# Order of weight products in pairs, split lag products and a new placing of intra-block products in a one-core encoder layer

## The chip, the cores and the metric

The kernel runs on one core of one Trainium2 chip. The metric is the device time of one execution in microseconds (us). The engines are TensorE (PE, with its weight loads shown apart as PEld), VectorE (DVE), ScalarE (ACT), GpSimd (POOL) and SyncE (SP), whose queue issues most DMAs.

## What is computed

One encoder layer on 256 tokens of width 2048, float32 throughout:

```python
q, k, v, u, g_att, g_ssm = jnp.split(x @ w_in, splits, axis=-1)   # 8 heads x 128; u: 64 groups x 16
y_att = neighbourhood_attention(q, k, v, rpb) @ w_na_out
y_s = s5_scan(u, forward) + s5_scan(u, reverse) + d * u            # 64 complex states per group
y_s = gelu(y_s); y_s = y_s * sigmoid(y_s @ w_glu + b_glu)
mix = (sigmoid(g_att + b) * y_att + sigmoid(g_ssm + b) * (y_s @ w_s5_out)) @ w_out
h = layer_norm(ALPHA * x + mix)
out = layer_norm(ALPHA * h + (silu(h @ w_gate) * (h @ w_up)) @ w_down)
```

## The kernel before

**Weights.** All weights come as one stream of tiles of 128x1024 floats. SP loads each into one of six slots of `raw` (`load`, line 328). ACT rounds it into one of four slots of `whi` (`split_hi`, line 580, the copy in line 585), and DVE writes the remainder, raw minus whi, over the raw tile as `wlo` (`split_lo`, line 1065, line 1068). Activations are kept in the same two parts, so a product is high x both parts plus low x high part.

**The product of a tile.** `prod_w` (lines 1727 to 1740) takes a tile as eight 128x128 stationary blocks: eight matmuls of 512 columns with `whi` (line 1734), then a wait for the tile's `wlo`, then eight of 256 columns with `wlo` (line 1738), into one PSUM bank. The last one raises `w_used`, on which three things wait: SP's load six tiles later, ACT's `split_hi` four tiles later, and the copies of the finished bank. An output of the input projection, or of the feed-forward's gate or up projection, takes two such tiles, one for each half of the 2048 inputs. `prod_b` (line 1742) and `prod_b_rows` (line 1755) use the activations as the stationary operand, 12 matmuls of 512 columns to a tile (lines 1750 to 1752, and 1769 to 1771).

**Stages in order.** The u projection (16 tiles, `U_ORDER`), the v projection (16 tiles, `prod_b`), the loop over eight heads `f` with `PER_F` = 12 tiles each (q, k and gates; lines 1919 to 1944), 40 tiles of branch projections, 32 of the output projection, layer norm with transposes (`h_part`, `h_pair`), the feed-forward's gate and up tiles (first twelve in `FF_ORDER`, then `ff(m)`, line 2057), 88 down tiles and the last norm.

**The state-space layer in the loop.** Time is cut into `Q` = 4 positions j of a block and `NB` = 64 blocks. Head f's step has three bursts of small float32 matmuls, placed by hand among the tiles j of the loop; each matmul of the code is two in the trace, called passes here:
- `s5_in(f)` (line 1850): 32 matmuls with 64 rows, 64 columns of weights, 64 columns streamed, on all four 64x64 positions of the array.
- `blocks(f)`: the kernels for lags -3 to 3. 16 matmuls (line 1829) with 128 rows and 32 weight columns, 7 lags x 16 = 112 columns streamed, into the four 32-partition strips of bank `WB`; rows 0 to 63 hold the forward direction and rows 64 to 127 the reverse one, and `cp` is zero where a direction has no lag. Then four small ones with the diagonal term (line 1832).
- `s5_out(f)`: eight matmuls within the blocks (line 1865), g = 0 on rows 0 to 63 and output partitions 0 to 63, g = 1 on rows 64 to 127 and partitions 64 to 127, then 32 with the block states (line 1874) on all four positions.

`s5_in(f+1)` and `blocks(f+1)` stand behind tile j = 10 of head f, `scores` and `s5_out` behind j = 7, `transposes` behind j = 11, `attend` behind j = 1 (for the last head, 5, 7, 9 and 10). ACT's `keep_lags` (line 645) copies the lags, ACT stores them and `y4` (`store_y`, two DMAs), and SP brings the lags back as `tb` (`stage_tb`). Everything on ACT and DVE is in an order written out by hand around the splits.

**Layer norm to feed-forward.** ACT runs `gain_even` (line 979), `pair_hi` (line 986) and the splits, DVE `gain_odd` (line 1593), `pair_low` (line 1072) and its own; `split_hi(0, H_FF + 4)` stands behind `pair_hi(5)` and `gain_even(7)`.

Of the kernel before, what the change touches and what calls it, by code (L numbers as in the profile page):

```python
# [28 lines left out]
P = 128  # L29
# [89 lines left out]
def build(nc, wstream, xT, xtok, b_rows, b_states, c_rows, d_rows, params, bias, cols, lnrows, out):  # L119
    ctx = ExitStack()  # L120
    with ctx:
# [84 lines left out]
        hi_ready, lo_ready, w_used = sem("hi_ready"), sem("lo_ready"), sem("w_used")  # L206
# [99 lines left out]
        def from_blocks(v):  # L306

            return v.rearrange("p (j r b) -> p b j r", j=Q, r=ROWS)

# [269 lines left out]
        def _(act):  # L579
            def split_hi(m, c):  # L580

                act.wait_ge(raw_landed[c % RING], 32 * m + 16 * (c // RING + 1))
                if not (isinstance(m, int) and 12 * m + c < HIS):
                    act.wait_ge(w_used, 12 * m + (c - HIS + 1))
                act.activation(whi[:, c % HIS, :], raw[:, c % RING, :], ACT.Copy).then_inc(hi_ready, 1)  # L585
# [54 lines left out]
            def keep_lags(f):  # L640
# [4 lines left out]
                act.activation(lags[:, :, :].rearrange("p m n -> p (m n)"), ps[WB][:, 0:7 * GC], ACT.Copy).then_inc(w_evac, 1)  # L645
                act.wait_ge(w_evac, f + 1)
# [4 lines left out]
            def store_y(f):  # L651

                act.wait_ge(fin_step, f + 1)
                for g in range(2):
                    act.dma_start(y_dram[f, :, GC * g:GC * g + GC, :],
                                  y4[64 * g:64 * g + 64, f % 2, :, :].rearrange("p q n -> p (q n)")).then_inc(y_stored, 16)

            def cross_y(f):

                act.wait_ge(y_done, f + 1)  # L660
                if f >= 2:
                    act.wait_ge(y_stored, 32 * (f - 1))
                act.activation(y4[:, f % 2, :, :].rearrange("p q n -> p (q n)"), y_bank(1), ACT.Copy).then_inc(y_cross, 1)

            def load_y(f):

                act.wait_ge(y_stored, 32 * f + 32)
# [396 lines left out]
        def _(dve):  # L1064
# [559 lines left out]
            split_lo(0, H_FF + 1)  # L1624
            gain_odd(4)
            split_lo(0, H_FF + 2)
# [93 lines left out]
        def _(pe):  # L1720
# [6 lines left out]
            def prod_w(m, c, act, k0, kn, bank, start, stop, ready=None, parts=False):  # L1727

                sh, sl = c % HIS, c % RING
                for i in range(kn):  # L1730
# [3 lines left out]
                    pe.matmul(bank[:, :], whi[:, sh, i * P:(i + 1) * P], both, start=start and i == 0, stop=stop and i == kn - 1,  # L1734
                              skip_group_check=parts)
                wait_split(m, c)
                for i in range(kn):
                    mm = pe.matmul(bank[:, 0:T], wlo[:, sl, i * P:(i + 1) * P], act[:, k0 + i, 0, :], start=False,  # L1738
                                   stop=stop and i == kn - 1, skip_group_check=True)
                mm.then_inc(w_used, 1)  # L1740

            def prod_b(c, act, k0, banks, start, stop):

                sh, sl = c % HIS, c % RING
                for n in range(2 * TT):
# [5 lines left out]
                    pe.matmul(banks[t][:, :], a, lo, start=False, stop=False)  # L1751
                    mm = pe.matmul(banks[t][:, :], b, hi, start=False, stop=stop and i == 1)  # L1752
                mm.then_inc(w_used, 1)

            def prod_b_rows(c0, act, k0, banks, between):

                for t in range(TT):
                    for m in range(SPL):
# [4 lines left out]
                        for i in range(2):  # L1763
# [6 lines left out]
                            pe.matmul(banks[t][:, :], a, lo, start=False, stop=False)  # L1770
                            mm = pe.matmul(banks[t][:, :], b, hi, start=False, stop=m == SPL - 1 and i == 1)  # L1771
                        if t == 1:
                            mm.then_inc(w_used, 1)
# [18 lines left out]

            pe.wait_ge(warm_ready, 1)
            keep_busy(ps[7], 7)
            for j, (n, h) in enumerate(U_ORDER):
                if h == 0:
                    wait_bank(N_U + n)
                if j == 0:
                    pe.wait_ge(half_hi, 1)
                else:  # L1800
                    wait_high(0, j)
                prod_w(0, j, act16, 8 * h, 8, ps[bank_of(N_U + n)], h == 0, h == 1,
                       x_split if n == 0 else None)
# [10 lines left out]
            def blocks(f):  # L1814
# [3 lines left out]
                else:  # L1818
                    pe.wait_ge(w_evac, f)
# [34 lines left out]
            def s5_out(f):  # L1854
# [7 lines left out]
                for q in range(4):  # L1862
# [317 lines left out]
```

## Time and profile before

| | us |
|---|---|
| median of 3 runs | 1366.38 (1365.68 to 1366.5) |
| the profiled execution's own time | 1366.87 |
| its span, first to last instruction | 1365.0 |
| PE busy in it | 1352.7 |
| DVE, ACT busy | 952.0, 680.9 |

The span is what the trace covers. Rows of the timeline give the start of a group in us from the span's start, how long it lasts until its last instruction ends, the engine, the line, the operation with its tiles and shape, and the count; an idle time before it with what ended it stands in brackets. Matmuls are pipelined: a matmul's duration overlaps that of the next, so the pace is read from start to start.

### The profile page before, as it was taken

To read this page: it belongs to the slowest core of one execution; us is meant where nothing else is said; L and a number is where in the kernel's file an instruction comes from. 1 tells how busy PE (TensorE), PEld (TensorE's weight loads), DVE (VectorE), ACT (ScalarE), POOL (GpSimd) and SP (SyncE) were. 2 spreads that over 40 slices of the span, in tenths; PEclk is the share of its full clock that TensorE was granted. 3 is DMA by queue.
4 is the path that set the end of the run, shared out by engine and by line. 5 is a ranking of instruction groups with operands and counts; after the bars stand their busy time and mean duration, and the time that the engine had idled before them with its cause. 6 is when DMAs were issued, how large, how long until landed. Compare 5 with 4: busy or idle time off the path is not lost.

```text
span 1365.0 us, 22724 instructions
## 1 busy us (share of the span) xinstructions
PE 1352.7 (99%) x8542; PEld 1164.4 (85%) x8542; DVE 952.0 (70%) x1291; ACT 680.9 (50%) x995; POOL 137.2 (10%) x207
## 2 busy tenths in 40 slices
PE   8999999999999999999999999999999999999998
PEld 7888888888888888888888888888888888888886
DVE  7989999999877797557666665555555554545454
ACT  5444555555548855347444444444444444333332
POOL 1842222220000000000222220000000000000001
PEclk9999999999999999999999999999999999999999
DMA  9667777676656676654656566566765666666663
GB/s 321 206 239 254 232 233 225 214 224 195 188 172 190 219 278 189 196 178 157 191 185 187 186 193 188 185 187 188 230 185 186 186 194 190 198 187 198 189 196 123
DMA packets 100797, 275.14 MB, mean 202 GB/s; under 512 B 25970, under 2 KB 33138, under 8 KB 100340
## 3 DMA queue, kind: packets, MB, share of 16 engines
q1 hardware_dynamic: 87364, 264.66, 61.5%
q10 hardware_dynamic: 9520, 5.54, 1.3%
q0 software_dynamic: 3840, 3.94, 1.0%
q8 instruction: 49, 0.80, 0.2%
q14 instruction: 24, 0.20, 0.1%
HBM read 268.12 MB, written 5.96 MB: 201 GB/s over the span
## 4 chain that ended last, share of the span: by engine, by line
PE 90%; DVE 6%; DMA 1%; SPq 1%; issue 1%; ACT 1%; DVEq 0%; ACTq 0%
PE bank L1734 41%; PE bank L1738 21%; PE bank L1750 8%; PE bank L1751 8%; PE bank L1752 8%; DVE wlo L1068 2%; DMA raw<-wstream 1%; DVE scratch L1094 1%; PE bank L1874 1%; PE bank L1850 1%; PE bank L1829 0%; PE bank L1771 0%; PE bank L1769 0%; PE bank L1770 0%; DVE scratch L1091 0%
## 5 line engine op out<-in xcount | busy, mean ns | idle before, releaser
L1068 DVE TENSOR_TENSOR wlo<-raw,whi 128x1024 fp32r<-128x1024 f32 x463 | 579.3, 1253 | 193.3 <-ACT whi L585 187.5
L585 ACT ACTIVATE whi<-raw 128x1024 fp32r<-128x1024 f32 x463 | 488.1, 1055 | 238.9 <-PE bank L1752 189.4
L1734 PE MATMUL bank<-act,whi 128*128 128x512 f32 x2280 | 575.8, 394 | 2.7 <-DVE act L1072 2.1
L1734 PEld LDWEIGHTS bank<-act,whi 128*128 128x128 f32 x2280 | 409.5, 189 | 78.6 <-DVE act L1072 4.1
L1738 PEld LDWEIGHTS bank<-act,wlo 128*128 128x128 f32 x2280 | 310.8, 190 | 25.4 <-DVE wlo L1068 3.2
L1738 PE MATMUL bank<-act,wlo 128*128 128x256 f32 x2280 | 318.1, 282 | 2.0 <-DVE wlo L1068 2.0
L1750 PE MATMUL bank<-whi,mid 128*128 128x512 f32 x340 | 132.3, 389 | 0.0
L1751 PE MATMUL bank<-wlo,mid 128*128 128x512 f32 x340 | 132.3, 389 | 0.0
L1752 PE MATMUL bank<-whi,mid 128*128 128x512 f32 x340 | 132.3, 389 | 0.0
L1654 DVE TENSOR_TENSOR usum<-bank,usum 128x256 f32<-128x256 f32 x44 | 18.7, 425 | 91.5 <-ACT usum L915 91.5
L915 ACT ACTIVATE usum<-bank 128x256 f32<-128x256 f32 x44 | 16.9, 384 | 126.9 <-PE bank L1738 126.9
L908 ACT ACTIVATE gsum<-bank 128x256 f32<-128x256 f32 x44 | 16.9, 384 | 118.8 <-PE bank L1738 118.8
L1750 PEld LDWEIGHTS bank<-whi,mid 128*128 128x128 f32 x340 | 63.8, 188 | 13.3
L1751 PEld LDWEIGHTS bank<-wlo,mid 128*128 128x128 f32 x340 | 63.8, 188 | 13.2
L1752 PEld LDWEIGHTS bank<-whi,mid 128*128 128x128 f32 x340 | 63.8, 188 | 13.2
L549 POOL DMA_DIRECT2D lrow<-lam_dram x120 | 57.1, 484 | 168.7 <-DVE tmp L1243 150.9
L1750 PE MATMUL bank<-whi,act 128*128 128x512 f32 x180 | 70.6, 392 | 0.2 <-DVE wlo L1068 0.2
L1751 PE MATMUL bank<-wlo,act 128*128 128x512 f32 x180 | 70.1, 389 | 0.0
L1752 PE MATMUL bank<-whi,act 128*128 128x512 f32 x180 | 70.1, 389 | 0.0
L1648 DVE TENSOR_TENSOR gsum<-bank,gsum 128x256 f32<-128x256 f32 x44 | 18.7, 425 | 69.2 <-ACT gsum L908 69.2
L563 POOL TENSOR_TENSOR hp<-hp,lnrow 128x512 f32<-128x512 f32 x8 | 18.8, 2348 | 410.6 <-DVE ev L1658 410.6
L573 POOL TENSOR_TENSOR hp<-hp,lnrow 128x512 f32<-128x512 f32 x2 | 2.5, 1266 | 538.6 <-ACT hp L1054 538.6
(200 smaller groups left out, 1158.9 us busy)
## 6 DMA issues: line engine op xcount, KB each, us to landing
raw<-wstream SPq DMA_DIRECT2D x463, 512.0 KB, 3.6
bt<-b_rows SPq DMA_DIRECT2D x8, 512.0 KB, 6.0
lrow<-lam_dram POOLq DMA_DIRECT2D x120, 32.0 KB
lnrow<-lnrows SPq DMA_DIRECT2D x3, 1024.0 KB, 7.0
xraw<-xT SPq DMA_DIRECT2D x8, 256.0 KB, 6.3
bs<-b_states SPq DMA_DIRECT2D x8, 256.0 KB, 5.4
hp<-xtok SPq DMA_DIRECT2D x4, 512.0 KB, 4.7
bm<-bias SPq DMA_DIRECT2D x8, 160.0 KB, 4.2
```

What stands on the lines that cost most here:

```text
L549: pool.dma_start(lrow[64 * g + j:64 * g + 64:Q, d, :, :, :].rearrange("p q r n -> p (q r n)"), row.to_broadcast([GC, 512])).then_inc(lrow_ ...
L563: pool.tensor_tensor(v, v, lnrow[:, 0, b], ALU.mult).then_inc(h_step, 1)
L585: act.activation(whi[:, c % HIS, :], raw[:, c % RING, :], ACT.Copy).then_inc(hi_ready, 1)
L908: act.activation(gsum[:, b, :], ps[bank_of(N_FF + 2 * i)][:, T:2 * T], ACT.Copy).then_inc(g_cross, 1)
L1068: dve.tensor_tensor(wlo[:, c % RING, :], raw[:, c % RING, :], whi[:, c % HIS, :].bitcast(F32), ALU.subtract).then_inc(lo_ready, 1)
L1648: dve.tensor_tensor(gsum[:, b, :], ps[bank_of(N_FF + 2 * i)][:, 0:T], gsum[:, b, :], ALU.add).then_inc(g_summed, 1)
L1654: dve.tensor_tensor(usum[:, b, :], ps[bank_of(N_FF + (2 * i + 1) % 6)][:, 0:T], usum[:, b, :], ALU.add).then_inc(u_summed, 1)
L1734: pe.matmul(bank[:, :], whi[:, sh, i * P:(i + 1) * P], both, start=start and i == 0, stop=stop and i == kn - 1, skip_group_check=parts)
L1738: mm = pe.matmul(bank[:, 0:T], wlo[:, sl, i * P:(i + 1) * P], act[:, k0 + i, 0, :], start=False, stop=stop and i == kn - 1, skip_group_che ...
L1750: pe.matmul(banks[t][:, :], a, hi, start=start and i == 0, stop=False)
L1751: pe.matmul(banks[t][:, :], a, lo, start=False, stop=False)
L1752: mm = pe.matmul(banks[t][:, :], b, hi, start=False, stop=stop and i == 1)
```

## The change

`prod_w` is cut into `high` (eight matmuls with `whi`, raising a new semaphore `hi_used`) and `low` (eight with `wlo`, raising `w_used`). In the head loop and in `ff` both tiles of an output are taken together: high, high, low, low. ACT's `split_hi` waits for `hi_used` and `lo_ready` instead of `w_used`. `blocks` takes each direction's three lags with 64 rows, into two banks, and the middle lag (zero) with all rows. `s5_out` places the products within the blocks of q = 2, 3 crosswise, so that they use all four positions. Three orders change: `s5_in` and `blocks` stand between the highs and the lows of the last pair, `split_hi(0, H_FF + 4)` and `split_lo(0, H_FF + 2)` stand earlier.

```diff
@@ lines 310 to 312
+        def y_rows(g, q):
+
+            h = g if q < 2 else 1 - g
+            return slice(64 * h, 64 * h + 64)
+
+        def lag_bank(f, d):
+
+            return ps[YB if f else AB][:, T:T + 3 * GC] if d else ps[WB][:, 4 * GC:7 * GC]
+
@@ split_hi, lines 582 to 585
-                    act.wait_ge(w_used, 12 * m + (c - HIS + 1))
+                    act.wait_ge(hi_used, 12 * m + (c - HIS + 1))
+                    act.wait_ge(lo_ready, 12 * m + (c - HIS + 1))
@@ keep_lags, lines 642 to 649
-                act.activation(lags[:, :, :].rearrange("p m n -> p (m n)"), ps[WB][:, 0:7 * GC], ACT.Copy).then_inc(w_evac, 1)
-                act.wait_ge(w_evac, f + 1)
+                act.activation(lags[:, Q - 1:2 * Q - 1, :].rearrange("p m n -> p (m n)"), ps[WB][:, 3 * GC:7 * GC], ACT.Copy).then_inc(w_evac, 1)
+                act.activation(lags[:, 0:Q - 1, :].rearrange("p m n -> p (m n)"), lag_bank(f, 1), ACT.Copy).then_inc(w_evac, 1)
+                act.wait_ge(w_evac, 2 * f + 2)
@@ store_y, lines 654 to 656
-                    act.dma_start(y_dram[f, :, GC * g:GC * g + GC, :],
-                                  y4[64 * g:64 * g + 64, f % 2, :, :].rearrange("p q n -> p (q n)")).then_inc(y_stored, 16)
+                    for q in (0, 2):
+                        act.dma_start(y_dram[f, :, GC * g:GC * g + GC, q * NB:q * NB + 2 * NB],
+                                      y4[y_rows(g, q), f % 2, q:q + 2, :].rearrange("p q n -> p (q n)")).then_inc(y_stored, 16)
@@ ACT, lines 990 to 995
                 pair_hi(g)
+                if g == 4:
+                    split_hi(0, H_FF + 4)
                 if g < 6:
                     gain_even(g + 2)
-                if g == 5:
-                    split_hi(0, H_FF + 4)
@@ DVE, lines 1624 to 1628
             split_lo(0, H_FF + 1)
+            split_lo(0, H_FF + 2)
             gain_odd(4)
-            split_lo(0, H_FF + 2)
@@ prod_b, lines 1750 to 1753 (prod_b_rows alike)
                     pe.matmul(banks[t][:, :], a, hi, start=start and i == 0, stop=False)
-                    pe.matmul(banks[t][:, :], a, lo, start=False, stop=False)
-                    mm = pe.matmul(banks[t][:, :], b, hi, start=False, stop=stop and i == 1)
-                mm.then_inc(w_used, 1)
+                    if n < 2 * TT - 1:
+                        pe.matmul(banks[t][:, :], a, lo, start=False, stop=False)
+                    mm = pe.matmul(banks[t][:, :], b, hi, start=False, stop=stop and n == TT)
+                mm.then_inc(hi_used, 1)
+                pe.matmul(banks[t][:, :], a, lo, start=False, stop=stop).then_inc(w_used, 1)
@@ blocks, lines 1826 to 1830
-                            pe.matmul(ps[WB][32 * q:32 * q + 32, 0:7 * GC], bs[:, r, 4 * g + q, :], cp[:, f % 2, r, 4 * g + q, :, :],
-                                      start=g == 0 and r == 0, stop=False, skip_group_check=True)
+                            for d in range(2):
+                                h = slice(64 * d, 64 * d + 64)
+                                c = cp[h, f % 2, r, 4 * g + q, (0 if d else Q):(Q - 1 if d else 2 * Q - 1), :]
+                                pe.matmul(lag_bank(f, d)[32 * q:32 * q + 32, :], bs[h, r, 4 * g + q, :], c.rearrange("p j n -> p (j n)"),
+                                          start=g == 0 and r == 0, stop=d == 1 and g == 1 and r == 1, skip_group_check=True)
+                for g in range(2):
+                    for r in range(2):
+                        for q in range(4):
+                            pe.matmul(ps[WB][32 * q:32 * q + 32, 3 * GC:4 * GC], bs[:, r, 4 * g + q, :], cp[:, f % 2, r, 4 * g + q, Q - 1, :],
+                                      start=False, stop=False, skip_group_check=True)
@@ s5_out, lines 1862 to 1866 (line 1874 writes to y_rows(g, q) too)
-                for q in range(4):
+                for q in (0, 2, 1, 3):
                     for g in range(2):
                         h = slice(64 * g, 64 * g + 64)
-                        pe.matmul(y_bank(g)[h, q * NB:q * NB + NB], tb[h, q, :, :].rearrange("p j n -> p (j n)"), u4[h, f % 2, q, :],
+                        pe.matmul(y_bank(g)[y_rows(g, q), q * NB:q * NB + NB], tb[h, q, :, :].rearrange("p j n -> p (j n)"), u4[h, f % 2, q, :],
@@ head loop, lines 1920 to 1944
+                for o in range(PER_F // 2):
...
+                    for i in range(2):
+                        high(0, c + i, act16, 8 * i, ps[bank_of(n)], i == 0)
+                    if f + 1 < KS and o == 5:
+                        s5_in(f + 1)
+                        blocks(f + 1)
+                    if o == 5 and f == HEADS - 1:
+                        attend(f)
+                    for i in range(2):
+                        low(0, c + i, act16, 8 * i, ps[bank_of(n)], i == 1)
@@ ff, lines 2057 to 2064
+                    for e in range(2):
+                        n, c = N_FF + 2 * i + e, H_FF + 4 * i + 2 * e
+                        pe.wait_ge(mid_ready if e else g_silu, 3 * m + (i - 2))
+                        for q in range(2):
+                            high(m, c + q, act16, 8 * q, ps[bank_of(n)], q == 0)
+                        for q in range(2):
+                            low(m, c + q, act16, 8 * q, ps[bank_of(n)], q == 1)
```

## Rows read from the trace of the kernel before

**Rows 1.** The page: busy time and share of the span.
```profile
PE 1352.7 (99%) x8542; PEld 1164.4 (85%) x8542; DVE 952.0 (70%) x1291; ACT 680.9 (50%) x995; POOL 137.2 (10%) x207
```
**Rows 2.** Timeline of PE in the feed-forward.
```profile
722.96 1.12 PE L1738 MATMUL bank<-act,wlo 128*128 128x256 f32 x8
723.91 2.00 PE L1734 MATMUL bank<-act,whi 128*128 128x512 f32 x8
725.75 1.11 PE L1738 MATMUL bank<-act,wlo 128*128 128x256 f32 x8
```
**Rows 3.** The down projection: busy us and instructions of each engine, clock, DMA.
```profile
1200.00:1300.00 100.00, 100.00 (x443) 82.80 (x442) 51.85 (x48) 38.79 (x37) 0.00 (x0) 1.00 0.62 193
```
**Rows 4.** Timeline of PE: the last low matmul of one tile.
```profile
115.75 0.28 PE L1738 MATMUL bank<-act,wlo 128*128 128x256 f32 x1
115.87 2.00 PE L1734 MATMUL bank<-act,whi 128*128 128x512 f32 x8
```
**Rows 5.** Timeline of PE behind tile 10 of head 6.
```profile
371.59 1.11 PE L1738 MATMUL bank<-act,wlo 128*128 128x256 f32 x8
372.63 1.16 PE L1850 MATMUL bank<-u,wb 64*64 64x64 f32 x64
373.73 0.97 PE L1829 MATMUL bank<-cp,bs 128*32 128x112 f32 x32
374.52 0.23 PE L1832 MATMUL bank<-dmat,ident 128*32 128x16 f32 x8
374.68 2.12 PE L1734 MATMUL bank<-act,whi 128*128 128x512 f32 x8
```
**Rows 6.** Timeline of PE: `s5_out` of head 7.
```profile
401.74 0.62 PE L1865 MATMUL bank<-u,tb 64*64 64x64 f32 x14
...
403.29 2.11 PE L1734 MATMUL bank<-act,whi 128*128 128x512 f32 x8
```
**Rows 7.** Timeline of ACT at the turn to head 7; then PE.
```profile
374.83 0.26 ACT L645 ACTIVATE lags<-bank 128x112 f32<-128x112 f32 x1 [3.55 <-PE bank L1832]
...
375.57 1.06 ACT L585 ACTIVATE whi<-raw 128x1024 fp32r<-128x1024 f32 x1 [0.48 <-ACT lags L645]
...
378.54 0.53 ACTq L655 DMA_DIRECT2D y_dram<-y  x1
...
384.28 0.51 PE L1734 MATMUL bank<-act,whi 128*128 128x512 f32 x1
```
**Rows 8.** Timeline of ACT in the feed-forward; then PE.
```profile
808.19 1.05 ACT L585 ACTIVATE whi<-raw 128x1024 fp32r<-128x1024 f32 x1
...
813.30 1.09 PE L1734 MATMUL bank<-act,whi 128*128 128x512 f32 x4
```
**Rows 9.** The page: DMA issues, count, KB each, median us to landing.
```profile
raw<-wstream SPq DMA_DIRECT2D x463, 512.0 KB, 3.6
```
**Rows 10.** Timeline of PE and of DVE, tiles 6 and 7 of head 0.
```profile
122.47 1.21 PE L1738 MATMUL bank<-act,wlo 128*128 128x256 f32 x8 [1.57 <-DVE wlo L1068]
...
125.37 1.10 PE L1738 MATMUL bank<-act,wlo 128*128 128x256 f32 x8
...
121.19 1.22 DVE L1068 TENSOR_TENSOR wlo<-raw,whi 128x1024 fp32r<-128x1024 f32 x1
...
123.87 1.22 DVE L1068 TENSOR_TENSOR wlo<-raw,whi 128x1024 fp32r<-128x1024 f32 x1
```
**Rows 11.** Timeline of PE, then ACT, then DVE, layer norm to feed-forward.
```profile
633.28 2.58 PE L1734 MATMUL bank<-act,whi 128*128 128x512 f32 x8 [0.52 <-ACT whi L585]
636.27 1.21 PE L1738 MATMUL bank<-act,wlo 128*128 128x256 f32 x8 [0.41 <-DVE wlo L1068]
...
629.81 0.56 ACT L979 ACTIVATE hT<-bank,col 128x256 f32<-128x256 f32 x1 [1.49 <-DVE act L1072]
...
632.18 1.04 ACT L585 ACTIVATE whi<-raw 128x1024 fp32r<-128x1024 f32 x1
...
634.99 3.49 DVE L1068 TENSOR_TENSOR wlo<-raw,whi 128x1024 fp32r<-128x1024 f32 x3
```

More of the change, by code:

```diff
@@ L205, in build @@
         raw_landed = [sem(f"raw_landed{i}") for i in range(RING)]
-        hi_ready, lo_ready, w_used = sem("hi_ready"), sem("lo_ready"), sem("w_used")
+        hi_ready, lo_ready, hi_used, w_used = sem("hi_ready"), sem("lo_ready"), sem("hi_used"), sem("w_used")
         uv_copied, loop_copied, res_added = sem("uv_copied"), sem("loop_copied"), sem("res_added")
@@ L1725, in wait_high, with high @@
                 pe.wait_ge(hi_ready, 12 * m + (c + 1))
-            def prod_w(m, c, act, k0, kn, bank, start, stop, ready=None, parts=False):
-                sh, sl = c % HIS, c % RING
-                for i in range(kn):
+            def high(m, c, act, k0, bank, start, ready=None):
+                sh = c % HIS
+                wait_high(m, c)
+                for i in range(8):
                     if ready:
@@ L1733, in prod_w, with low @@
                     both = act[:, k0 + i, :, :].rearrange("p h n -> p (h n)")
-                    pe.matmul(bank[:, :], whi[:, sh, i * P:(i + 1) * P], both, start=start and i == 0, stop=stop and i == kn - 1,
-                              skip_group_check=parts)
+                    mm = pe.matmul(bank[:, :], whi[:, sh, i * P:(i + 1) * P], both, start=start and i == 0, stop=False,
+                                   skip_group_check=True)
+                mm.then_inc(hi_used, 1)
+            def low(m, c, act, k0, bank, stop):
+                sl = c % RING
                 wait_split(m, c)
-                for i in range(kn):
+                for i in range(8):
                     mm = pe.matmul(bank[:, 0:T], wlo[:, sl, i * P:(i + 1) * P], act[:, k0 + i, 0, :], start=False,
-                                   stop=stop and i == kn - 1, skip_group_check=True)
+                                   stop=stop and i == 7, skip_group_check=True)
                 mm.then_inc(w_used, 1)
@@ L1791, in keep_busy, with first_high @@
                     pe.matmul(bank[:, 0:T], S[:, 0, 0:P], S[:, 0, 0:T], start=True, stop=True)
+            def first_high(bank):
+                for k in range(8):
+                    x_split(k)
+                    both = act16[:, k, :, :].rearrange("p h n -> p (h n)")
+                    mm = pe.matmul(bank[:, :], whi[:, 0, k * P:(k + 1) * P], both, start=k == 0, stop=False, skip_group_check=True)
+                mm.then_inc(hi_used, 1)
             pe.wait_ge(warm_ready, 1)
@@ L1818, in blocks @@
                 else:
-                    pe.wait_ge(w_evac, f)
+                    pe.wait_ge(w_evac, 2 * f)
                 if f == 0:
@@ L1939, in _ @@
                         transposes(f)
-                    if f + 1 < KS and j == 10:
-                        s5_in(f + 1)
-                        blocks(f + 1)
-                    if j == 10 and f == HEADS - 1:
-                        attend(f)
             def last_head(kt):
@@ L2014, in hi_part @@
                 for k in range(k0, k0 + 4):
-                    pe.matmul(o, whi[:, (H_FF + c) % HIS, k * P:(k + 1) * P], act16[:, k, :, rows], start=t == 0 and k == 0,
+                    mm = pe.matmul(o, whi[:, (H_FF + c) % HIS, k * P:(k + 1) * P], act16[:, k, :, rows], start=t == 0 and k == 0,
                                    stop=False, skip_group_check=True)
+                if m == 3:
+                    mm.then_inc(hi_used, 1)
             def low_part(c):
```

66 lines of the change are left out of this document (28 added, 38 removed).

## The prediction

> **What bounds the kernel.** I read the page first: PE is busy for 1352.7 of 1365.0 us, DVE for 952.0, ACT for 680.9 [rows 1]. So time is won or lost where PE's own sequence gets shorter or longer, or where PE stands still; work on the other engines counts only if it makes PE wait. The timeline of PE, read from start to start, then gives the prices. In the feed-forward a tile is 2.79 us: the eight high matmuls take 1.84 us (723.91 to 725.75), the eight low ones 0.95 [rows 2]. There is no idle time in it. The down projection, in which all matmuls have 512 columns, holds 443 in 100 us, up to two of them only partly, so one is 0.2265 us and eight are 1.81 [rows 3]: eight highs behind a run of lows cost 0.03 more than eight in an even run. Lows run at 0.12 apiece (115.75 to 115.87) [rows 4], eight of them would be 0.96, and a run of eight behind highs takes 0.95, so the first is 0.01 short. A turn from lows to highs and back thus costs 0.02 net. Nothing says that a wait on a semaphore costs anything when it is fulfilled: rows 3 has one in every twelve matmuls.
>
> **Part 1, two tiles together.** The change takes away one of two turns for each output: 6 in each of 8 heads, and 2 for each of 41 outputs of the feed-forward (44 less the three of the first twelve tiles), 130 in all. 130 x 0.02 = **2.6 us** less. Nothing is added to PE: the same 32 matmuls, and increments. Ends: 0, if 16 lows in a row leave a debt twice as large as eight do; 130 x 0.03 = 3.9, if the first low's 0.01 is not lost. I take the middle, since the runs of far denser passes before a high block leave hardly more (the eight highs that follow `blocks` last 2.12 us to the end of the last, those that follow a run of eight lows 2.00 [rows 4, 5], and the turn of tile shape, below, is 0.09 or more of it).
>
> What the pairs ask of the others, costed at nothing:
> - The second high of a pair is wanted 0.95 us earlier (at 1.84 instead of 2.79 into the pair), and tile 11 of a head 0.95 + 2.05 = 3.0 us earlier, as `s5_in` and `blocks` now follow it. ACT's `whi` is ready 7.65 us ahead in a late place of a head (done at 376.63, used at 384.28) [rows 7], with the same order of work in each head, and in the feed-forward the first `whi` of a step of four tiles is done at 809.24 and used at 813.30, 4.1 us ahead [rows 8]. That cover is enough. If it were gone, PE would stand still for the excess, at each pair.
> - `w_used` of a pair's first tile comes at 4.6 instead of 2.79, so SP issues that load 1.8 us later, with the loads queued behind it on SP; the slot is used again three pairs on, 16.8 us after the pair's start. 4.6 + 3.6 to land [rows 9] + 1.05 on ACT = 9.3. Covered by 7 us.
> - `split_hi` waits for `hi_used`, at 1.84 where `w_used` came at 2.79 (3.66 against 5.59 for the second), and for `lo_ready` of the tile four back, which DVE finished before PE could have used it; behind this wait stands all of ACT's order, and it is never later than before unless DVE is.
> - `blocks` ends 1.0 us later, so ACT, which stood 3.55 us for it before `keep_lags`, stands 4.5, with the split behind it [rows 7]: 7.65 us ahead becomes 6.6. The second copy of the lags (0.26 us each) and two more y stores (0.53 us each to issue) [rows 7] come out of the same cover.
>
> **Part 2, products within the blocks.** `s5_out` lasts from 401.74 to 403.29, 1.55 us [rows 6], `s5_in` from 372.63 to 373.73, 1.10 [rows 5]. All passes have 64 columns. In `s5_in` each of four positions takes 16 passes. In `s5_out` two positions take 8 + 16 = 24 and the others 16, so eight more in a position cost 0.45 us, 0.056 each. After the change each position has 4 + 16 = 20: four less on the longest, 0.225 per head, **1.8 us** over 8. Ends: 0 (if the new order lets two passes on one position follow each other) and 1.8.
>
> **Part 3, the lags.** `blocks` now: 0.95 us (373.73 to 374.68), of which 0.79 is for 32 passes, eight on each of four strips [rows 5]; so 0.099 for a pass of 112 columns. Between 64 columns (0.056) and 112 lies 0.9 ns a column, so a pass of 48 would stream in about 0.042 and one of 16 in about 0.015. After the change there are 64 passes of 48 columns on eight positions (eight each), then 32 of 16 columns on four (eight each), then the eight of line 1832 as before. Streaming alone: 8 x 0.042 = 0.34 and 8 x 0.015 = 0.12. But there are now 96 passes where 32 were, and there may be a least time per pass. The eight passes of line 1832 take 0.16 with the turn of shape behind them [rows 5]. A turn of shape is 0.09: the eight lows before `s5_in` take 1.04 instead of 0.95 (371.59 to 372.63). That leaves 0.07 over eight, 0.008 per pass at most. At 0.007, 64 passes are 0.45 and 32 are 0.22. Then comes one more turn of shape, from 64 rows to 128, of 0.09 to 0.15, and the 0.16 of the end. Sum: 0.45 + 0.22 + 0.12 + 0.05 (the first pass on each position has to be loaded) + 0.16 = 1.00 to 1.05, that is 0.07 more than now: **0.6 us** over 8 heads, more. Ends: streaming alone 0.34 + 0.12 + 0.12 + 0.05 + 0.16 = 0.79 (1.3 us less over 8); and the mean start-to-start of `s5_in`'s passes, 1.10 / 64 = 0.017, taken as the least: 96 x 0.017 + 0.33 = 1.96, 1.0 more per head, 8 us over 8. I take the 0.007 because line 1832 is the only row with passes shorter than 64 columns, while `s5_in` is explained by its streaming (16 x 0.056 and a start).
>
> **Part 4, layer norm to feed-forward.** PE waits for `whi` of tile H_FF + 4 (0.52) and then for its `wlo` (0.41) [rows 11]. ACT makes that `whi` at 632.18, and does `pair_hi(6)` only after it, but it stood idle for 1.49 us before 629.81, and I take it that the tile was there by then. Moved up, the split fills that hole and `pair_hi(6)` starts at about 632.3, as soon as the gains before it are done, 0.8 earlier; with it come DVE's two `pair_low` and its split, at 634.2 instead of 634.99, and PE's lows at 635.5 instead of 636.27. **0.75 us** less. Ends 0 and 0.9 (then the `wlo` of the next tiles would be what is late). DVE's `split_lo(H_FF + 2)` is moved past one 0.5 us operation that waited for PE anyway: nothing.
>
> **Part 5, head 0.** DVE is late once in the loop: PE waits 1.57 us for the `wlo` of tile 6, there at 122.41, then uses tile 7's at 125.37, ready at 125.1 [rows 10]. In pairs PE would want tile 6's low only at 122.35, so that wait goes; but tile 7's is late next: lows 7 would be wanted at 123.4 and start at 125.1. So of 1.57 only **0.3 us** is won. Ends 0 and 1.7.
>
> **Sum.** -2.6 - 1.8 + 0.6 - 0.75 - 0.3 = -4.85. Against the profiled execution's 1366.87 (its span 1365.0 and 1.9 around it) that is 1362.0; it stands 0.5 above the median of the runs, so I forecast **1361.5 us**. A difference of 0.2%, 2.7 us, is about what a measurement here can tell from none.
>
> **Rivals.**
> - Pairs bring nothing: the debt of 0.02 belongs to the lows, not to the turn. Against it: the small extra behind `blocks`. For it: no row has 16 lows in a row. 1361.5 + 2.6 = 1364.1.
> - Short passes are bound by their number. PE would have a least time from one pass to the next; each head pays it 96 times in `blocks`. The other parts win 5.45 us, 0.68 per head, so it decides from 0.95 + 0.68 = 1.63 us for `blocks`, (1.63 - 0.33) / 96 = 0.0135 us per pass. The present `blocks` has 0.79 / 32 = 0.025 from pass to pass, explained by its columns but also by such a floor if `s5_in`, at 0.017, were of another kind. At 0.017 the time is 1361.5 + 7.4 = 1368.9, at 0.025 it is 96 x 0.025 + 0.33 = 2.73, 1.78 more per head, 1361.5 + 13.6 = 1375.
>  The Trainium skill, page "TensorE: Matmul & The Clock Gate", section on the measured gap of 56 ns, has such a rule: start-to-start never drops below about 25 ns, however few columns. By it this change would be slower, at 1375. The trace does not agree for tiled float32 passes, 64 in 1.10 us [rows 5].
> - A new wait: the later `w_used` or the moved `blocks` makes ACT or the ring late, and PE waits once in each of seven heads. Against it: 4 to 7 us of cover. A wait of 0.7 each gives 1366.4.
> - More is won: head 0's wait goes altogether and `blocks` streams freely, 1361.5 - 1.4 - 1.9 = 1358.2.
>
> **Chances.** Forecast 0.58, more won 0.08, pairs bring nothing 0.14, short passes 0.13 (0.08 slower by over 0.2%, 0.05 within), a new wait 0.07 (0.02 of it slower). The case of pairs lies at -2.3, at the edge of 0.2%: 0.03 of it counts as faster. So faster 0.69, within 0.2% 0.21, slower 0.10. The range reaches from just inside the case of more won, 1358.5, over that of a new wait into that of the short passes, 1367.2; beyond it lie most of the short passes' 0.13 and little else.
>
> **What would show it.** Right: high groups of 16 with 1.84 + 1.81 us and lows with 1.91, an output of the feed-forward at 5.57 instead of 5.59; `s5_out` at 1.32 instead of 1.55; `blocks` at 1.0; the low group of H_FF + 4 0.75 earlier; no new releaser among PE's waits. Wrong: an output still at 5.59 (first rival), `blocks` above 1.6 (second), a wait of PE on line 585's or line 1068's result in heads 1 to 7 (third).

## The result and the profile after

| | before | after |
|---|---|---|
| median of 20 runs, us | 1366.65 | 1368.12 |
| lowest to highest, us | 1365.68 to 1367.28 | 1367.26 to 1371.68 |
| profiled execution, us (span) | 1366.87 (1365.0) | 1371.68 (1369.8) |

The ratio is 1.0014, with a 95% interval of 1.0009 to 1.002: some 1.5 us slower, where 4.9 us less was forecast. The prediction was wrong; the result lies above its range. The runs of after also spread over 4.4 us, those of before over 1.6, and the profiled execution is the slowest of them: its idle times are larger than those of the median run.

The page, busy times [rows 1] and the load's landing [rows 9]:

```profile
PE 1353.7 (99%) x9054; PEld 1167.0 (85%) x9054; DVE 951.5 (69%) x1291; ACT 683.1 (50%) x1003; POOL 137.3 (10%) x207
...
raw<-wstream SPq DMA_DIRECT2D x463, 512.0 KB, 4.3
```

PE has 512 more matmuls, as 64 more passes in each of 8 heads should give. Loads take 4.3 us from issue to landing instead of 3.6. ACT waits longer for them than before (37.7 us in all, before 19.6), PE never. Of PE's waits the following matter here (tile and line that waited, what ended the wait: us in total, times, longest):

```profile
PE bank L1867 <- issue: 2.1, 2, 1.7
PE bank L1747 <- ACT whi L595: 2.1, 1, 2.1
PE bank L1756 <- DVE wlo L1080: 1.7, 2, 1.3
...
PE bank L1756 <- issue: 1.0, 1, 1.0
```

Line 1747 is the matmul of `high`, 1756 that of `low`, 1862 a direction's lags, 1867 the middle lag, 1870 the diagonal. The first, second and fourth row are new. "issue" means that the profile shows nothing that PE waited for. The timeline of PE shows the steps. First the feed-forward [rows 2]:

```profile
722.63 2.08 PE L1756 MATMUL bank<-act,wlo 128*128 128x256 f32 x16
724.55 3.82 PE L1747 MATMUL bank<-act,whi 128*128 128x512 f32 x16
728.20 2.08 PE L1756 MATMUL bank<-act,wlo 128*128 128x256 f32 x16
```

From start to start the 16 lows take 1.92 and the 16 highs 3.65: 5.57 for an output, as forecast. One output can't show 0.02 us, but the mean over some 70 of them can: 5.587 before, 5.567 after. Then head 2 around `blocks` [rows 5], and `s5_out` of head 7 [rows 6]:

```profile
216.00 1.16 PE L1888 MATMUL bank<-u,wb 64*64 64x64 f32 x64
217.09 0.81 PE L1862 MATMUL bank<-cp,bs 64*32 64x48 f32 x64
217.83 0.45 PE L1867 MATMUL bank<-cp,bs 128*32 128x16 f32 x32
218.10 0.26 PE L1870 MATMUL bank<-dmat,ident 128*32 128x16 f32 x8
218.29 1.93 PE L1756 MATMUL bank<-act,wlo 128*128 128x256 f32 x14
...
405.62 0.46 PE L1903 MATMUL bank<-u,tb 64*64 64x64 f32 x16
405.91 1.11 PE L1912 MATMUL bank<-sb,cp 64*64 64x64 f32 x64
406.95 3.24 PE L1747 MATMUL bank<-act,whi 128*128 128x512 f32 x13
```

`blocks` lasts 1.20 us (217.09 to 218.29), 0.74 for the directions, 0.27 for the middle lag and 0.19 for the end; forecast were 0.50, 0.34 and 0.16. `s5_out` lasts 1.33 instead of 1.55, as forecast. In head 6 the same passes are interrupted:

```profile
375.69 0.43 PE L1867 MATMUL bank<-cp,bs 128*32 128x16 f32 x28
377.82 0.21 PE L1867 MATMUL bank<-cp,bs 128*32 128x16 f32 x2 [1.70 <-issue]
...
378.05 3.54 PE L1756 MATMUL bank<-act,wlo 128*128 128x256 f32 x16
```

The profile shows no semaphore event that ends that wait. What else happens there shows in the view of the DMA queues for the window 374 to 377 us:

```profile
DMA packets 1, 0.02 MB, mean 5 GB/s; under 512 B 0, under 2 KB 0, under 8 KB 0
...
q8 instruction: 1, 0.02, 3.2%
```

The only packet is a piece of the program, on the queue of instructions (in the view's 40 slices it lies at 374.8 to 374.9; its record is 1.51 us long). Two more such stalls are in the trace, each with such a read just ahead: in head 1 PE stands idle for 0.4 us until 178.79, and in head 4 for 1.0 us until 298.83, among the lows right behind `blocks`. In all three PE starts again 1.4 us after the end of the read's record, which is 2.4 to 2.9 us after its start. After the long one, of 1.7 us, the 16 lows take 3.3 us instead of 1.9. The windows 378.10:381.30 and 381.50:385.00 (after the busy times and counts of PE, PEld, DVE, ACT and POOL comes the granted clock, then the DMA share and GB/s):

```profile
378.10:381.30 3.20, 3.20 (x18) 3.20 (x17) 1.67 (x3) 1.38 (x3) 0.00 (x0) 0.54 0.22 37
381.50:385.00 3.50, 3.50 (x18) 2.71 (x17) 2.96 (x5) 1.74 (x4) 0.00 (x0) 0.96 0.76 240
```

Last, the wait for `whi`. It lies behind the last head, where no row of the prediction was taken. The timeline of PE, ACT and ACT's queue, branch projections:

```profile
416.94 0.70 PE L1939 MATMUL bank<-PT,vcur 128*128 128x160 f32 x4
417.68 0.38 ACT L747 ACTIVATE act8a<-bank 128x256 fp32r<-128x256 f32 x1 [2.82 <-PE bank L1939]
417.79 0.52 ACTq L667 DMA_DIRECT2D y_dram<-y  x1
418.35 1.63 ACTq L667 DMA_DIRECT2D y_dram<-y  x3
424.88 1.87 ACTq L681 DMA_DIRECT2D u<-y_dram  x4
431.04 1.06 ACT L837 ACTIVATE u<-u 128x1024 f32<-128x1024 f32 x1 [2.91 <-DMA u<-y_dram]
434.49 1.04 ACT L595 ACTIVATE whi<-raw 128x1024 fp32r<-128x1024 f32 x1
435.68 3.13 PE L1747 MATMUL bank<-act8a,whi 128*128 128x512 f32 x8 [2.05 <-ACT whi L595]
```

The same chain before:

```profile
412.43 0.71 PE L1901 MATMUL bank<-PT,vcur 128*128 128x160 f32 x4
413.56 0.53 ACTq L655 DMA_DIRECT2D y_dram<-y  x1
414.13 0.53 ACTq L655 DMA_DIRECT2D y_dram<-y  x1
418.01 0.31 ACTq L669 DMA_DIRECT2D u<-y_dram  x1
423.65 1.06 ACT L825 ACTIVATE u<-u 128x1024 f32<-128x1024 f32 x1 [2.16 <-DMA u<-y_dram]
```

By head 7 the whole trace of after is already behind: `s5_out` starts at 405.62, before at 401.74 [rows 6]. Counted from that start, `attend(7)` comes 0.6 us later than before, the first load of y 3.0 us and `gelu` 3.5 us. The four stores take 2.2 us to issue (from 417.79 to 419.98), the two of before 1.1. ACT's order puts PE's next `whi` behind `gelu`. The eight highs at 435.68 take 3.13 instead of 2.00.

### The profile page after: what moved, and what is told of

It is laid out like the page before. It is cut to its first block, busy times and chain, and to the rows that moved or that the text cites. A ratio compares the mean times of both kernels' runs of the same rounds, so it can differ in the third digit from the quotient of the medians.

```text
span 1369.8 us, 23940 instructions
## 1 busy us (share of the span) xinstructions
PE 1353.7 (99%) x9054; PEld 1167.0 (85%) x9054; DVE 951.5 (69%) x1291; ACT 683.1 (50%) x1003; POOL 137.3 (10%) x207
## 4 chain that ended last, share of the span: by engine, by line
PE 88%; DVE 6%; DMA 2%; SPq 1%; issue 1%; ACT 1%; ACTq 0%; DVEq 0%
PE bank L1747 39%; PE bank L1756 21%; PE bank L1768 8%; PE bank L1771 8%; PE bank L1770 6%; DVE wlo L1080 2%; PE bank L1773 2%; DMA raw<-wstream 1%; DVE scratch L1106 1%; PE bank L1888 1%; PE bank L1912 1%; ACT whi L595 0%; PE bank L1789 0%; PE bank L1792 0%; PE bank L1862 0%
## 5 line engine op out<-in xcount | busy, mean ns | idle before, releaser
L1747 PE MATMUL bank<-act,whi 128*128 128x512 f32 x2272 | 546.8, 392 | 0.0
L1747 PEld LDWEIGHTS bank<-act,whi 128*128 128x128 f32 x2272 | 416.5, 188 | 81.0 <-DVE act L1084 0.3
L1756 PEld LDWEIGHTS bank<-act,wlo 128*128 128x128 f32 x2280 | 294.6, 192 | 15.2 <-DVE wlo L1080 2.3
L1756 PE MATMUL bank<-act,wlo 128*128 128x256 f32 x2280 | 300.4, 284 | 2.7 <-DVE wlo L1080 1.7
L1770 PE MATMUL bank<-wlo,mid 128*128 128x512 f32 x255 | 99.2, 389 | 0.0
L1770 PEld LDWEIGHTS bank<-wlo,mid 128*128 128x128 f32 x255 | 47.9, 188 | 9.8
L1770 PE MATMUL bank<-wlo,act 128*128 128x512 f32 x135 | 52.6, 389 | 0.0
```

The source lines that it names most:

```text
L1747: mm = pe.matmul(bank[:, :], whi[:, sh, i * P:(i + 1) * P], both, start=start and i == 0, stop=False, skip_group_check=True)
```

## The experiments

Two questions: which part costs, and why. "Before" in an edit is the kernel before the change, "after" the changed one. Every ratio is to the kernel before, on the same chip.

**Parts alone.** `a1_pairs`: before, with tiles in pairs and the bursts and `attend` at their new places; lags, intra-block products and the two reordered splits as before.

```diff
+                    for i in range(2):
+                        high(0, c + i, act16, 8 * i, ps[bank_of(n)], i == 0)
+                    if f + 1 < KS and o == 5:
+                        s5_in(f + 1)
+                        blocks(f + 1)
...
-                    act.wait_ge(w_used, 12 * m + (c - HIS + 1))
+                    act.wait_ge(hi_used, 12 * m + (c - HIS + 1))
```

> The kernel before with the pairs alone (high and low split, both tiles of an output together in the head loop and the feed-forward, s5_in, blocks and the last attend between highs and lows). Theory S (the loss is made by the dense short passes of blocks and by the late y chain, the pairs are sound): 2.5 us below before from the turns, some 0.3 more in head 0, so 1363.9, and an output of the feed-forward at 5.57 us. Rival P (the later release of the weight ring or the moved bursts cost what the turns give): 1365.5 or more, with PE waits on whi or on issue that the kernel before does not have.

`a2_lags`: before, with the new `blocks` and `keep_lags` alone.

```diff
+                            for d in range(2):
+                                h = slice(64 * d, 64 * d + 64)
+                                c = cp[h, f % 2, r, 4 * g + q, (0 if d else Q):(Q - 1 if d else 2 * Q - 1), :]
```

> The kernel before with the split lags alone. Theory S: blocks takes 1.20 us instead of 0.95, 2.0 us over 8 heads, and PE stands idle for issue once or twice behind it (0.6 to 1.9 us each), so 1369.5 with a wider spread of runs than before's 1.6 us. Rival P (blocks costs what its passes show and no more): 1368.6, no idle time of PE for issue.

`a3_intra`: before, with the crosswise products of `s5_out` and their four stores alone.

```diff
-                for q in range(4):
+                for q in (0, 2, 1, 3):
...
-                                      y4[64 * g:64 * g + 64, f % 2, :, :].rearrange("p q n -> p (q n)")).then_inc(y_stored, 16)
+                                          y4[y_rows(g, q), f % 2, q:q + 2, :].rearrange("p q n -> p (q n)")).then_inc(y_stored, 16)
```

> The kernel before with the crosswise intra-block products and their four y stores alone. If they gain what s5_out shows, 0.22 us per head: 1364.9. Theory S holds that the two added stores delay the last load of y, and with it ACT and the first projection, only together with the later attend: so 1364.9 and no wait of PE on whi there. Rival (the stores alone do it): 1367 to 1369, PE waits about 2 us on whi in the branch projections and the granted clock falls behind it.

`a4_old_lags`: after, with the lags undone.

```diff
-                            for d in range(2):
-                                h = slice(64 * d, 64 * d + 64)
...
+                            pe.matmul(ps[WB][32 * q:32 * q + 32, 0:7 * GC], bs[:, r, 4 * g + q, :], cp[:, f % 2, r, 4 * g + q, :, :],
```

> The kernel after the change with blocks and keep_lags as before. Theory S with the lags as the main loss: 2.0 us for the passes and about 1.2 for the idle times go: 1364.9, or 1361.9 if the wait on whi in the branch projections was a part of the slowest run alone. Rival (the y chain is the main loss and recurs in every run): 1366 or more, with PE waiting 2 us on whi near 433 us. Rival P: 1367.5.

| | median, us (range) | ratio, 95% |
|---|---|---|
| before | 1366.62 | |
| a1_pairs | 1365.01 (1363.79 to 1367.78) | 0.9987 (0.9979 to 0.9996) |
| a2_lags | 1371.18 (1370.72 to 1376.85) | 1.0041 (1.0028 to 1.0054) |
| a3_intra | 1364.93 (1363.72 to 1365.99) | 0.9987 (0.9978 to 0.9995) |
| a4_old_lags | 1363.54 (1362.61 to 1365.99) | 0.9981 (0.9972 to 0.999) |

Split lags alone cost 4.6 us, where 0.6 was forecast; everything else together wins 3.1. `a1_pairs` wins 1.6 us (interval 0.5 to 2.9), less than the 2.7 expected; in its trace PE has a new wait of 0.9 us for `whi`. `a2_lags` is 1.7 us slower than its theory said. `a3_intra` came out as expected. The stalls belong to the lags. The waits of `a2_lags` (line 1842 is its middle lag) show

```profile
PE bank L1842 <- issue: 1.6, 2, 1.1
```

in heads 1 and 6, behind the same 14th and 28th pass of the middle lag as in after; `a1_pairs`, `a3_intra` and `a4_old_lags` have no such row. The wait for `whi` belongs to the pairs: 0.9 us in the branch projections of `a1_pairs`, none there in `a3_intra`, 1.3 in `a4_old_lags`, which has the later `attend` and the four stores:

```profile
427.90 1.39 PE L1746 MATMUL bank<-act8a,whi 128*128 128x512 f32 x5 [1.30 <-ACT whi L595]
```

**The last head.** `b1_old_lags_early_y` is `a4_old_lags` with head 7's stores of y issued inside the head, before `attend` is waited for, and the load of y two tiles earlier; `b2_early_y` is the same edit on after.

```diff
+                            store_y(f)
...
-                    store_y(HEADS - 1)
+                    load_y(HEADS - 1)
...
-                if j == 3:
-                    load_y(HEADS - 1)
```

> The kernel after the change with blocks and keep_lags as before, and with the last head's y stored before its pt_copy and loaded back two tiles sooner. Theory Y (the later attend and the two added stores make the last load of y late, ACT stands for it and PE then waits for whi in the branch projections, 1.3 to 2 us, in every run): the wait of PE on whi near 427 us is gone, 1.4 below a4_old_lags, 1362.1. Rival (that wait is there in some runs only, or something else is late next on ACT): 1363.5, or a wait of PE in the same stage on another result.

> The kernel after the change, with the same early store and load of the last y. Theory Y: 2 to 4 us below the profiled execution of after, in the median 1.5 to 2 below its 1368.1, so 1366.4; what then stands between it and b1_old_lags_early_y is the split lags alone, 4.3 us (2.0 for their passes, the rest idle time of PE for issue). Rival: 1368, the split lags and the y chain do not add up.

`b3_early_y_apart`: `b2_early_y` with `s5_in` behind the first high of the pair and `blocks` behind the second, so that 64 and 104 passes stand where 168 stood in a row.

```diff
-                    if f + 1 < KS and o == 5:
-                        s5_in(f + 1)
-                        blocks(f + 1)
+                        if f + 1 < KS and o == 5:
+                            (s5_in, blocks)[i](f + 1)
```

> As b2_early_y, with s5_in behind the first high of the last pair and blocks behind the second, so that eight matmuls of 512 columns (1.8 us) stand between the two dense bursts. Theory S (PE runs out of instructions where the reading of a new piece of 16 KB of program falls into 168 passes in a row; the reading takes about 2.4 us): no idle time for issue of 0.5 us or more in the loop, 1 to 2 us less, against 0.2 more per head for the two more turns of tile shape, 1.4 in all, so about b2_early_y with a narrower spread. Rival (the idle times belong to blocks itself, or to a semaphore): the idle times stay and the time is 1.4 above b2_early_y.

`b4_order`: before, with only the two splits moved up.

```diff
+                if g == 4:
+                    split_hi(0, H_FF + 4)
...
-                if g == 5:
-                    split_hi(0, H_FF + 4)
```

> The kernel before with the two reordered splits between layer norm and feed-forward alone. The prediction's step: the lows of tile H_FF + 4 begin 0.75 us sooner, 1365.9. Rival (the place is bound by what DVE and ACT do before): 1366.6, the gap of PE before them unchanged.

| | median, us (range) | ratio, 95% |
|---|---|---|
| before | 1366.84 | |
| b1_old_lags_early_y | 1360.92 (1360.67 to 1361.81) | 0.9959 (0.9946 to 0.9973) |
| b2_early_y | 1366.12 (1365.37 to 1368.27) | 0.9996 (0.9987 to 1.0005) |
| b3_early_y_apart | 1364.79 (1363.88 to 1367.36) | 0.9986 (0.9977 to 0.9995) |
| b4_order | 1365.97 (1364.84 to 1367.03) | 0.9994 (0.9985 to 1.0003) |

The early stores win 2.6 us without the new lags (1363.54 to 1360.92) and 2.0 with them (1368.12 to 1366.12; 3.0 and 2.5 by the ratios). In `b1_old_lags_early_y` PE waits neither for `whi` nor for issue; it is the fastest kernel here that computes the whole layer, 1.2 us faster than its theory said. The lags cost 5.2 between `b1` and `b2`. With the passes apart 1.3 comes back (the intervals of `b2` and `b3` overlap); the waits, first of `b2_early_y`, then of `b3_early_y_apart`:

```profile
PE bank L1755 <- issue: 1.4, 1, 1.4
PE bank L1866 <- issue: 1.2, 1, 1.2
```

```profile
PE bank L1866 <- issue: 0.6, 1, 0.6
```

The stall in head 6 stands at the same pass in all five kernels with the whole new `blocks`. In `b2_early_y`, as in after, it follows the 28th of the middle lag's 32:

```profile
378.41 0.43 PE L1866 MATMUL bank<-cp,bs 128*32 128x16 f32 x28
379.99 0.21 PE L1866 MATMUL bank<-cp,bs 128*32 128x16 f32 x2 [1.15 <-issue]
```

The same holds of the other places: in head 4 PE stops behind the eighth low in after, `b2` and `d2` (below). What changes from kernel to kernel is how long it stands, and each of the ten stalls of 0.4 us or more in these five traces ends 1.3 to 1.4 us after the end of a read of the program. PE thus stops at fixed points of its program, and goes on some time after a read. This is the strongest sign for the read as the cause.

**What the apart placing costs, and head 0.** `c1_best_apart` is `b1` with the edit of `b3`. `c2_best_head0` is `b1` with DVE's build of the next head's factors, in head 0, moved behind tile 7's split.

```diff
-                    if j == 5 and f == 0:
+                    if j == 7 and f == 0:
...
-                    if j == 6 and f + 1 < KS:
+                    if j == (6 if f else 7) and f + 1 < KS:
```

> b1_old_lags_early_y with s5_in behind the first high and blocks behind the second of the last pair. There is no idle time for issue in b1, so only the two more turns of tile shape show: 0.2 per head in seven heads, 1.4 above b1's 1360.9, 1362.3. Then the distance from b2 to b3 (1.3 less) would be 2.7 of idle time less 1.4 of turns. Rival (a turn of shape inside a run of highs costs next to nothing, or the bursts apart free something else): within 0.5 of b1.

> b1_old_lags_early_y with form_b(1) of head 0 moved on DVE behind the remainder of tile 7 instead of before that of tile 6. The step of the prediction on head 0 (DVE's own chain decides, the wait only moves from tile 6 to tile 7): PE's wait of 1.6 us at the lows of tile 7 goes, 1359.3. Rival (the rows of lrow for head 2 then come later through GpSimd's queue and DVE stands for them at the end of the head, so that a later remainder is late): 1360.9 or more, with a wait of DVE on lrow near 136 us and a wait of PE on wlo after it.

`c1_best_apart` took 1362.76 (1362.03 to 1363.08; ratio 0.9968, 0.9956 to 0.9981): 1.8 more than `b1`, with two more turns in each of 7 heads. The traces give the part of the turns: from the `s5_in` behind head 2's tiles to the next one it is 38.90 us in `b1` and 39.12 in `c1`, 0.22 per head and 1.5 in all. The 1.3 that `b3` gains on `b2` thus come after turns that cost 1.5 to 1.8, so its idle time must be some 3 us less in the medians. `c2_best_head0` took 1366.11 (1363.89 to 1368.55; ratio 0.9993, 0.9984 to 1.0002), and its rival was right: the wait on tile 7 goes, but DVE then stands before the operation that reads `lrow`, whose loads are issued 7 us later than in `b1` (from 135.06 instead of 128.04), with the remainders queued behind. The view names no event that ended DVE's wait; that it was these loads follows from the code's order. DVE's timeline in head 0, and PE's row of waits:

```profile
141.87 1.23 DVE L1252 TENSOR_TENSOR pt<-bt,lrow 128x1024 f32<-128x1024 f32 x1 [4.21 <-issue]
...
PE bank L1754 <- DVE wlo L1078: 5.9, 5, 2.3
```

**What a pass costs.** `d1_no_middle` is `b2` with the 32 products of the middle lag left out (its output lacks the products of lag zero and keeps only the diagonal term there). `d2_one_half_first` is `b2` with the loop over directions outside that over q, so that four passes in a row use one half of the rows.

```diff
-                for g in range(2):
-                    for r in range(2):
-                        for q in range(4):
-                            pe.matmul(ps[WB][32 * q:32 * q + 32, 3 * GC:4 * GC], bs[:, r, 4 * g + q, :], cp[:, f % 2, r, 4 * g + q, Q - 1, :],
```

> b2_early_y without the products of the middle lag (the 32 passes of 16 columns are left out, so lag 0 holds the diagonal term alone). Theory S (behind the first 32 passes, each pass costs some 8.5 ns whatever its columns, and the idle time for issue comes with the number of passes in a row): blocks takes 0.27 less, 2.2 us over 8 heads, and of the two idle times one or both go, so 1362 to 1364. Rival (the turn from 64 to 128 rows is what costs): the diagonal products keep that turn, so the gain per head is under 0.2 and the idle times stay, 1365.

```diff
-                        for q in range(4):
-                            for d in range(2):
+                        for d in range(2):
+                            for q in range(4):
```

> b2_early_y with the four strips of the forward direction issued before the four of the reverse one instead of in turns. Theory S (the supply of passes is the bound behind the first 32): the 64 passes keep 0.74 us, within 0.03, and the time stays at 1366.1. Rival (the two row halves hold each other up when their passes alternate): the 64 passes change by 0.1 or more per head, the time by 1 us or more.

`d1_no_middle` took 1360.41 (1360.21 to 1361.49; ratio 0.9953, 0.9939 to 0.9966), `d2_one_half_first` 1366.53 (1365.14 to 1368.49; 0.9997, 0.9988 to 1.0006). PE in head 2 of `d1_no_middle`:

```profile
216.21 0.81 PE L1861 MATMUL bank<-cp,bs 64*32 64x48 f32 x64
216.94 0.26 PE L1864 MATMUL bank<-dmat,ident 128*32 128x16 f32 x8
217.13 2.17 PE L1755 MATMUL bank<-act,wlo 128*128 128x256 f32 x16
```

and of `d2_one_half_first`:

```profile
216.57 0.81 PE L1861 MATMUL bank<-cp,bs 64*32 64x48 f32 x64
217.31 0.44 PE L1866 MATMUL bank<-cp,bs 128*32 128x16 f32 x32
```

The 64 passes take 0.73 and 0.74 in either order, so what holds them is not whether neighbours use the same half of the rows. Without the middle lag `blocks` is 0.28 shorter, 2.2 us over 8 heads; the kernel is 5.7 shorter than `b2` (5.9 by the ratios), 1.6 below the range of its theory. It has no wait for issue at all, and its 5 runs spread over 1.3 us, the 11 of `b2` over 2.9. But the edit also shortens the program, so that the reads fall at other places: in head 6 one starts 2.7 us behind the start of `s5_in`, where `b2` has it at 1.0. The run doesn't tell fewer passes from other places. In `d2_one_half_first` the stalls are still there, and the median with them:

```profile
PE bank L1866 <- issue: 1.4, 1, 1.4
...
PE bank L1755 <- issue: 0.8, 1, 0.8
```

## Why the prediction was wrong

**Pairs (-2.6): right.** An output of the feed-forward takes 0.020 us less in the mean, and a head 0.13 us less (39.26 us before, 39.13 in `a1_pairs`, from the `s5_in` behind head 2's tiles to the next), which is 0.02 for each of its six turns. So the debt belongs to the turn and not to the lows; the rival "pairs bring nothing" is out. The run of the pairs alone won only 1.6 us in the median; 0.9 us of the rest is the new wait for `whi`, which belongs to the step "costed at nothing".

**Intra-block products (-1.8): right.** `s5_out` is 0.22 shorter, a head takes 39.03 us in `a3_intra` instead of 39.26, and the run measured -1.7 (interval -3.0 to -0.7).

**Layer norm to feed-forward (-0.75): right in kind, sized too small.** `b4_order` measured -0.9, but its interval reaches from -2.1 to +0.4, so the median alone shows nothing. In its trace the wait of 0.52 for `whi` is gone and one of 0.40 for `wlo` is left, as forecast:

```profile
631.67 2.11 PE L1734 MATMUL bank<-act,whi 128*128 128x512 f32 x8
634.18 1.22 PE L1738 MATMUL bank<-act,wlo 128*128 128x256 f32 x8 [0.40 <-DVE wlo L1068]
```

From the first highs of the feed-forward to these lows it takes 5.39 us where it took 6.54, so the place gave 1.1, more than the upper end of 0.9. The eight highs, which took 2.58 [rows 11], take 2.11 now.

**Head 0 (-0.3): right in kind.** The wait of 1.57 [rows 10] has moved to tile 7's low. It is 1.31 in after's trace, and 1.45 in `b1`'s, so 0.1 to 0.3 was won:

```profile
124.67 1.22 PE L1756 MATMUL bank<-act,wlo 128*128 128x256 f32 x8 [1.31 <-DVE wlo L1080]
```

These four parts with the chain of y mended are `b1_old_lags_early_y`: -5.9 measured (interval -7.4 to -3.7), -5.45 forecast.

**The lags (+0.6): this step failed, in two ways.** The first is a size. The term "64 passes are 0.45", with 0.05 for the first loads, which no row showed, was mis-sized: the 64 passes take 0.74. I had taken 0.007 per pass from eight passes behind a turn, and streaming for the rest. `blocks` became 1.20 us, not 1.0: 0.25 more than before, 2.0 us over 8 heads. The traces agree, with 39.14 us for a head in `b2` and 38.90 in `b1`. (Two slips are in the working: the terms add up to 1.00, which is 0.4 us more over 8 heads and not 0.6, and the line through 64 and 112 columns gives 0.013 for 16 columns, not 0.015. Neither matters beside the miss.)

The rest of the 5.2 us, some 3 us, is the second way, and my bounds had no name for it: PE stands idle for 0.4 to 1.7 us at a time with nothing that the profile shows it waiting for. The runs show that this comes with the new `blocks`, in 1 to 3 of the 8 heads of a trace, always at the same points of the program and always behind a read of the program. They do not show that the number of passes in a row decides: bursts of 168 passes stall in some heads and not in others, `b3_early_y_apart` stalls once with 104 in a row, and `d1_no_middle` never with 136. The old bursts of 104, with 112 columns in `blocks`, never stall, though such reads lie beside them too (in `b1` one starts 0.2 us ahead of `s5_in` in head 1). I take it that PE has instructions in store while a read is under way, that short passes use the store up faster than it is filled, and that it shows where the store ends inside or right behind a dense burst. That fits the shorter stall of `b3_early_y_apart`, with eight highs ahead of `blocks`. It is read from the traces, and no run moves the reads while it leaves the passes alone. The rival, that the kernels without a stall only have their reads at luckier places, is open.

The number of instructions does cost, as in the rival "short passes are bound by their number", but not by a least time of 0.0135 us or more: the middle lag runs at 0.27 / 32 = 0.0084. That the measured 1368.1 came out near that rival's lower price, 1368.9, is luck: the lags cost 4.6 more than forecast, part of it in stalls, and the chain of y gave the other 2. The Trainium skill's rule of that rival (page "TensorE: Matmul & The Clock Gate", the section on the 56 ns gap: start-to-start never below about 25 ns) doesn't hold for these passes, by a factor of three.

**"Costed at nothing": this step failed too.** I wrote that the moved bursts and "two more y stores" come out of a cover of 6.6 us. That cover was read at the turn from head 6 to head 7 [rows 7], and "the same order of work in each head" is not true of the last: there `attend(7)` is in the place of the bursts, ACT waits for it before it stores y, and the load, `gelu` and the next `whi` all stand behind the store. The rival "a new wait" spoke of 0.7 us in each of seven heads; it came once, 2.1 us long in the profiled execution, and it is worth 2.0 (after less `b2_early_y`) to 2.6 us (`a4_old_lags` less `b1`). The later `attend` alone makes 0.9 of the wait (`a1_pairs`), the four stores alone make none (`a3_intra`), and both together 1.3 (`a4_old_lags`). In the heads the cover held, as forecast: after has no wait of PE on ACT there.

**The sum by the runs:** -5.9 (pairs, intra-block, order, head 0) + 5.2 (lags) + 2.0 (chain of y) = +1.3; measured +1.5. The three are the steps of one path, before to `b1` to `b2` to after, so they must add up but for the scatter of before; the sum says how the loss is shared, and is no proof of the causes.

**Open:** what holds the 64 passes at 0.74 us; why PE resumes some 1.4 us after the end of a read; and how often the median run stalls. Each profile is one execution: in the median some 3 us of the lags' cost are not passes, while in the four profiles with 168 passes in a row the rows of waits for issue sum to 1.6 to 3.1.

## What to carry to other kernels

Cost a burst of small matmuls by its number of instructions as well as by its columns, and look for "issue" among PE's waits: in these traces PE stood still in and right behind dense bursts of short passes. Spreading over more positions paid where the number of passes stayed the same (`s5_out`), and lost where it took three short passes in place of each one of 112 columns (`blocks`). A cover read in the middle of a loop says nothing about the last iteration: follow the moved step through the place where the loop's order ends. Here the best version keeps the old lags, and stores y before it waits for the attention.

## What the hardware showed that was not expected

- **Pace of small passes.** Start to start, the middle lag's passes (16 columns) run at 0.27 / 32 = 0.0084 us; the 64 passes of 48 columns take 0.0115 each with the turn of shape and the first load among them.
- **Idle time of PE beside reads of the program.** Stalls of 0.4 to 1.7 us in PE with no event that ends them, in all five profiled kernels with the whole of the new `blocks` (104 passes), in none of the others, and 1.3 to 1.4 us from the end of a read to the next matmul. On 512 more matmuls (9054 for 8542) the page counts 53 reads of the program for 49.
- **Clock.** After the stall of 1.7 us (head 6) the granted clock is at 0.54 for the next 3.2 us, the level of 1.2 GHz; after the wait of 2.1 us in the branch projections it is at 0.50 again, before it returns to 2.4 GHz:

```profile
436.50:439.60 3.10, 3.10 (x11) 2.62 (x10) 2.11 (x4) 3.10 (x8) 0.00 (x0) 0.50 0.04 16
441.00:444.00 3.00, 3.00 (x18) 2.64 (x17) 3.00 (x6) 3.00 (x6) 0.00 (x0) 1.00 0.58 175
```

After the stall of 1.0 us in head 4 it stayed at 1.00. In `b2_early_y` it was at 0.50 (from 121.6 to 124.9) after a wait of 1.9 us for `wlo` in head 0, and not after its two stalls of 1.2 and 1.4, so a part of what that profile is above its median has nothing to do with the lags. So a long idle time of PE can be paid almost twice: behind the stall of 1.7 us the 16 lows take 3.3 us instead of 1.9.
